# Hybrid mixer and product-key expert layer on one core: three old pairs of expert rows leave the chain of the first picks, in block 1 towards the mixer and in block 7 to behind it

## The chip, the cores and the metric

The kernel is one program on one core of a Trainium2 chip. The metric is the device time of one execution, in microseconds. All arithmetic is float32.

## The reference, cut to what matters

The input is 1024 tokens of width 1024. A mixer (sliding-window attention in one half, gated DeltaNet in the other) gives x1 by a layer norm, and then each token retrieves experts:

```python
def one_block(xb):                                  # 128 tokens
    q = (xb @ w_query).reshape(L, PEER_HEADS, 2, PEER_QUERY_DIM // 2)
    s = jnp.einsum('lhpd,hpkd->lhpk', q, sub_keys)  # 8 heads x 2 lists of 128 keys
    vals, idx = lax.top_k(s, K)                     # 16 best of each list
    cand = (vals[..., 0, :, None] + vals[..., 1, None, :]).reshape(L, PEER_HEADS, K * K)
    ...
    best, pos = lax.top_k(cand, K)                  # 16 best of 256 candidates
    expert = jnp.take_along_axis(cidx, pos, axis=-1)
    gate = jax.nn.softmax(best, axis=-1)
    u = expert_u[expert]                            # 8 heads x 16 picks = 128 rows a token
    v = expert_v[expert]
    h = jax.nn.gelu(jnp.einsum('ld,lhkd->lhk', xb, u), approximate=False)
    return jnp.einsum('lhk,lhkd->ld', (h * gate).astype(xb.dtype), v)
```

A second layer norm over x1 and this sum gives the output.

## The kernel before, in words

The tokens are worked on in NB = 8 blocks of 128 (blocks 0 to 7). For each block n the routine `mix(n, ...)` runs on four engines, each in its own fixed order:

- the mixer proper: rope, attention scores, softmax, convolution taps, the powers and merges that solve the triangular system, the state update (`ws0`, `kv0`, `ws1`, `kv1`), the output projection (`out0` to `out3`), and the first layer norm (`scale1`, `shift1`, `x1_T`);
- the query product: eight chunks of the query weights on PE (line 641), in four parts of two chunks, each followed by a product with the sub-keys (line 1018);
- the picks: DVE takes the 16 best of each key list and the 16 best of the candidates (lines 1547 to 1562), for four groups of lists, numbered 0 to 3. Group 0, "the first picks", ends with the expert numbers of the first 32 slots being written into `expert_used` (line 1906, which raises the semaphore `staged`).

A block has 128 slots, that is PAIRS = 64 pairs. For each slot GpSimd issues one indirect DMA (line 567) that brings 128 rows of u and v, 8 KB each, into one of the RING = 10 places of `ring`. So 5 pairs are on their way or waiting at once, and the gather of slot j waits until slot j - 10 has been added into the sum (`added`); the gathers of a new block wait for `staged` as well. A pair is then worked off in three steps: DVE takes two products with x1 (line 1933), ACT applies gelu and gate and writes two small diagonal matrices (lines 1398 to 1405), PE adds the pair into `expert_sum` (line 1062, 8 products).

The pairs of a block are spread over the work of the block itself and of the next one. Each named point of `mix` is a mark; a table says how many pairs are worked off at it. Marks up to `pick0` take "old" pairs, those of block n - 1 (`EARLIER`); from `top1` on they take "own" pairs, of block n (`OWN`, 15 of them; 23 in block 0, 30 in block 7). DVE and ACT take the pairs of a mark at the mark, PE takes them up to one pair less (`experts(n - 1, b - 1)`) and the last one in `turn_over`. So the order of all work around the picks is a table written by hand:

```python
scale1=1, shift1=1, x1_T=1, half_q=1, qu0=1, top0=1, more0=1, sel0=1, rest0=1, pick0=1,
...
FEWER = ("scores", "softmax", "att_o", "pow2", "solve", "kv0", "dn", "out1")
SECOND_EARLIER = {name: count - (name in FEWER) for name, count in EARLIER.items()}
```

`EARLIER` has 49 old pairs and serves blocks 2 to 7; `SECOND_EARLIER` has 41 and serves block 1, since block 0 works off 23 of its own. The order of DVE from there on is: pair of `half_q`; pair of `qu0`; wait for the first key scores (line 1344, ACT); first half of the 16 best; pair of `top0`; second half; pair of `more0`; candidates and first half of their 16 best; pair of `sel0`; second half; pair of `rest0`; expert numbers, `staged`; pair of `pick0`; then `turn_over`, which waits until PE has added the last old pair, reads the sums (line 1951) and sets x1 in place for the own pairs. PE's order is: query chunks 0 and 1 with the first key scores; then at the marks of the same names: `qu0`, query chunks 2 and 3, `top0`, key scores, `more0`, chunks 4 and 5, `sel0`, key scores, `rest0`, chunks 6 and 7, `pick0`, key scores, `turn_over`. ACT copies each result on between PE and DVE, in the same order. SP loads the weights in halves of a chunk, 512 KB, into four places (line 523); a load waits until the half four places before it has been used. After the query weights of a block SP goes on with weights for the input projection of the next blocks (`pass_steps`); block 7 has none.

With 64 pairs in a block, the last old pair is pair 64; the marks `half_q`, `qu0`, `top0`, `more0`, `sel0`, `rest0`, `pick0` take pairs 58 to 64 before the change.

Of the kernel before, what the change touches and what calls it, by code (L numbers as in the profile page):

```python
# [30 lines left out]
NB = SEQ // P  # L31
# [93 lines left out]
def constants():  # L125
# [24 lines left out]
EARLIER = dict(  # L150
    rope=1, gates=1, taps1=1, scores=2, taps2=1, softmax=2, turn_p=2, att_o=2,
    norms=1, decay=1, kk=1, aT=1, pow2=2, pow4=1, pow8=1, prod3=1, turn32=1, merge32=1, turn64=1,
    merge64=1, solve=2, ws0=1, kv0=2, ws1=1, kv1=1, dn=2, o_T=1, out0=1, out1=1, out2=1, out3=1,
    scale1=1, shift1=1, x1_T=1, half_q=1, qu0=1, top0=1, more0=1, sel0=1, rest0=1, pick0=1,
)
# [3 lines left out]
OWN = {name: 1 for name in ("top1",) + NEXT_IN + AFTER_IN}  # L159
LAST_OWN = {name: 2 for name in OWN}  # L160
FIRST_OWN = {name: 2 if name in ("top1", "more1", "sel1", "rest1", "pick1", "top2", "sel2", "pick2") else 1 for name in OWN}
FEWER = ("scores", "softmax", "att_o", "pow2", "solve", "kv0", "dn", "out1")
SECOND_EARLIER = {name: count - (name in FEWER) for name, count in EARLIER.items()}


def own_of(n):
# [1 line left out]


def earlier_of(n):  # L170
    return SECOND_EARLIER if n == 1 else EARLIER


assert sum(EARLIER.values()) + sum(OWN.values()) == PAIRS and 2 * sum(OWN.values()) <= PART
assert sum(SECOND_EARLIER.values()) + sum(FIRST_OWN.values()) == PAIRS and 2 * sum(FIRST_OWN.values()) <= 2 * PART

# [5 lines left out]
class Marks:  # L182
# [3 lines left out]
    def __init__(self, n, earlier=None, own=None, behind={}):  # L186
        self.names, self.behind, self.own_pairs, self.earlier_pairs = list(EARLIER) + list(OWN), behind, own_of(n), earlier_of(n)
        self.earlier, self.own, self.done = earlier, own, sum(own_of(n - 1).values()) if n else 0
# [1863 lines left out]
```

## Time and profile before

| | |
|---|---|
| time, median of 3 runs | 3087.7 us (3087.36 to 3089.36) |
| the profiled execution | 3080.46 us, its span 3078.7 us |
| busy: PE, DVE, ACT, POOL | 76%, 73%, 37%, 39% of the span |
| indirect gathers | 1024, 1073.81 MB, 84.3% of the 16 DMA engines' time |
| weights and other loads | 154.58 MB, 12.7% |
| all DMA | 1235.90 MB, mean 401 GB/s over the span |

The DMA engines are busy nearly all of the span and no engine is; so a reader looks first for the stretches where the DMA engines were not busy, and for what the gathers waited for there. All times given as "at 494.49" are us from the start of the span.

### The profile page before, as it was taken

The page shows a single profiled execution, that of the slowest core. Times are in us where ns is not written, and L with a number is a line of the kernel's source. Part 1 is how long each engine was busy: PE and PEld are TensorE (multiplying, and loading weights), DVE is VectorE, ACT ScalarE, POOL GpSimd, SP SyncE. Part 2 cuts the span into 40 slices and gives each one's busy share as a digit, 9 for nine tenths or more (in the row PEclk, how much of TensorE's full clock was granted, in tenths as well). Part 3 has the DMA queues.
Part 4 walks back from the last instruction along what each step waited for, and adds up shares of the span by engine and source line. Part 5 has one row for each costly group of instructions (what it writes and reads, how often), then busy time and mean ns, then how long its engine had stood idle before and what let it go on. Part 6 is the DMA issues. An engine that isn't in the chain of part 4 may idle for free.

```text
span 3078.7 us, 37919 instructions
## 1 busy us (share of the span) xinstructions
PE 2348.2 (76%) x11834; PEld 1325.7 (43%) x11834; DVE 2241.4 (73%) x5663; ACT 1127.5 (37%) x3546; POOL 1188.6 (39%) x1028
## 2 busy tenths in 40 slices
PE   8987888867798777877778787876878767775555
PEld 7764445524365343543345343542435434341111
DVE  5577766986679765897658966698657976678644
ACT  4233533354323633235323353324432263323222
POOL 0042452345433353234532445234443344434442
PEclk9999899879899898988989889998988889887777
DMA  8199999999999999999999999999999999999997
GB/s 352 68 401 418 420 420 399 411 415 420 420 417 417 410 421 420 396 413 419 420 419 407 418 419 420 404 406 412 420 420 402 418 416 420 420 378 421 421 421 318
DMA packets 189144, 1235.90 MB, mean 401 GB/s; under 512 B 21768, under 2 KB 21896, under 8 KB 54800
## 3 DMA queue, kind: packets, MB, share of 16 engines
q0 software_dynamic: 147456, 1073.81, 84.3%
q1 hardware_dynamic: 39312, 154.58, 12.7%
q10 hardware_dynamic: 2176, 5.10, 0.4%
q8 instruction: 95, 1.56, 0.2%
q14 instruction: 105, 0.86, 0.1%
HBM read 1229.21 MB, written 4.19 MB: 401 GB/s over the span
## 4 chain that ended last, share of the span: by engine, by line
DVE 30%; PE 29%; DMA 25%; ACT 7%; issue 7%; POOL 3%; DVEq 0%; SPq 0%; POOLq 0%; ACTq 0%
DMA ring<-in_uv,expert_used 24%; DVE ring L1933 13%; PE expert_sum L1062 13%; PE bank L641 7%; POOL ring L567 3%; PE bank L648 2%; ACT diag L1405 2%; PE bank L630 2%; DVE arena L1547 1%; DVE conv L1567 1%; DVE arena L1866 1%; DVE arena L1869 1%; DVE arena L1562 1%; ACT arena L1196 1%; DVE arena L1556 1%
## 5 line engine op out<-in xcount | busy, mean ns | idle before, releaser
L567 POOL DMA_INDIRECT ring<-in_uv,expert_used x1024 | 1188.4, 1161 | 1857.8 <-PE expert_sum L1062 1378.5
L1062 PE MATMUL expert_sum<-ring,diag 128*64 128x512 f32 x4096 | 1187.9, 709 | 632.2 <-ACT diag L1405 631.3
L1933 DVE CUSTOM_DVE_ANT_0 ring<-ring,x_pair 128x1024 f32<-128x1024 f32 x1024 | 1225.9, 1222 | 461.5 <-DMA ring<-in_uv,expert_used 456.9
L1062 PEld LDWEIGHTS expert_sum<-ring,diag 128*64 128x64 f32 x4096 | 311.5, 155 | 1255.9 <-issue 1241.2
L1398 ACT ACTIVATE h_raw<-h_raw 128x2 f32<-128x2 f32 x512 | 104.1, 203 | 1443.4 <-DVE h_raw L1933 1442.1
L1405 ACT ACTIVATE diag<-const,h_raw 128x64 f32<-128x64 f32 x1024 | 292.8, 333 | 9.2 <-PE expert_sum L1062 9.1
L1401 ACT ACTIVATE h_raw<-h_raw,gate_used 128x1 f32<-128x1 f32 x1024 | 245.6, 286 | 16.7
L641 PEld LDWEIGHTS bank<-oT,chunk 128*128 128x128 f32 x1344 | 152.7, 192 | 22.7 <-issue 22.7
L641 PE MATMUL bank<-oT,chunk 128*128 128x128 f32 x1344 | 158.6, 277 | 0.0
L1547 DVE MAX8 arena<-arena 128x8 f32<-128x128 f32 (+1 forms) x384 | 104.2, 325 | 31.2 <-ACT arena L1344 25.1
L630 PE MATMUL bank<-chunk,oT 128*128 128x256 f32 x464 | 109.7, 387 | 0.0
L630 PEld LDWEIGHTS bank<-chunk,oT 128*128 128x128 f32 x464 | 85.6, 190 | 40.5 <-issue 30.3
L641 PEld LDWEIGHTS bank<-o_cat,chunk 128*128 128x128 f32 x768 | 92.2, 200 | 22.1 <-issue 22.1
L1398 ACT ACT_TABLE_LOAD x76 | 97.5, 1283 | 3.6 <-DVE h_raw L1933 2.3
L648 PEld LDWEIGHTS bank<-arena 128*128 128x128 f32 x640 | 78.9, 198 | 41.6 <-issue 38.2
L641 PE MATMUL bank<-o_cat,chunk 128*128 128x128 f32 x768 | 96.6, 286 | 0.0
L648 PE MATMUL bank<-arena 128*128 128x128 f32 x640 | 88.6, 289 | 1.3 <-ACT arena L1289 0.6
L1339 ACT COPY arena<-bank 128x512 f32<-128x512 f32 (+1 forms) x33 | 18.9, 573 | 180.5 <-PE bank L641 180.5
L1933 DVE DVE_READ_ACCUMULATOR2_ANT h_raw<- 128x1 f32 x1024 | 83.5, 82 | 0.0
L1567 DVE SCALAR_TENSOR_TENSOR conv<-conv_in,conv_w,conv 128x128 f32<-128x128 f32 x288 | 77.6, 342 | 0.0
L641 PEld LDWEIGHTS bank<-xT_even,chunk 128*128 128x128 f32 x576 | 67.1, 195 | 13.8 <-issue 13.8
L641 PE MATMUL bank<-xT_even,chunk 128*128 128x128 f32 x576 | 70.1, 281 | 0.0
(289 smaller groups left out, 2652.4 us busy)
## 6 DMA issues: line engine op xcount, KB each, us to landing
chunk<-in_weights SPq DMA_DIRECT2D x228, 512.0 KB, 8.4
ring<-in_weights SPq DMA_DIRECT2D x17, 1024.0 KB, 23.5
ring<-in_uv,expert_used POOLq DMA_INDIRECT x1024, 15.2
chunk<-in_weights SPq DMA_DIRECT2D x4, 1024.0 KB, 20.5
x<-in_x SPq DMA_DIRECT2D x8, 512.0 KB, 14.9
o_cat<-in_xT SPq DMA_DIRECT2D x7, 512.0 KB, 14.1
out<-oT ACTq DMA_DIRECT2D x7, 512.0 KB, 9.3
xT_even<-in_xT SPq DMA_DIRECT2D x4, 512.0 KB, 10.2
```

The lines of the kernel that those rows point to most:

```text
L567: pool.indirect_dma_start(out=place(n, j), out_offset=None, in_=io["uv"], in_offset=bass.IndirectOffsetOnAxis(ap=expert_used[:, j:j + 1], ...
L630: mm = pe.matmul(out, act[:, k, :], w[:, k % 4, :], start=(k == ks[0]), stop=(k == ks[-1]))
L641: mm = pe.matmul(out, w[:, k % 4, i * P:(i + 1) * P], act[:, k, :], start=(k == 0), stop=(k == KT - 1))
L648: mm = pe.matmul(out[:, hs], lhsT[:, hs], rhs[:, hs], start=True, stop=True)
L1062: mm = pe.matmul(expert_sum[i][c * SPAN:(c + 1) * SPAN, :], diag[:, (j % DIAGS) * SPAN:(j % DIAGS + 1) * SPAN], place(n, j)[:, D + i * 512 ...
L1196: act.activation(pr, pr, ACT.Exp, bias=col(S_NMAX + h), accum_out=col(S_SUM + h)).then_inc(probs.sem, 1)
L1398: act.activation(h_raw[:, pair[0]:pair[1] + 1], h_raw[:, pair[0]:pair[1] + 1], ACT.Gelu).then_inc(gelued.sem, 1)
L1401: act.activation(h_raw[:, j:j + 1], h_raw[:, j:j + 1], ACT.Copy, scale=gate_used[:, j:j + 1]).then_inc(weighted.sem, 1)
L1405: act.activation(diag[:, (j % DIAGS) * SPAN:(j % DIAGS + 1) * SPAN], C["halves"], ACT.Copy, scale=h_raw[:, j:j + 1]).then_inc(diag_ready.s ...
L1547: ins = dve.max(values[:, one[part]], one[2])
L1567: stt(out=convo[:, t, :], in0=conv3[n % 2][:, t, k:k + P], scalar=conv_w[:, t * TAPS + k:t * TAPS + k + 1], in1=convo[:, t, :], op0=ALU.mu ...
L1933: dve.tensor_tensor_reduce(u, u, x_pair[:, (j % 2) * D:(j % 2 + 1) * D], 1.0, 0.0, ALU.mult, ALU.add, h_raw[:, j:j + 1]).then_inc(dotted.s ...
```

## The change

Two tables are changed, and nothing else: no instruction is added or removed, only the places of pairs of lines 1933, 1398 to 1405 and 1062 in the engines' orders change.

```diff
-FEWER = ("scores", "softmax", "att_o", "pow2", "solve", "kv0", "dn", "out1")
+FEWER = ("softmax", "att_o", "solve", "dn", "out1", "qu0", "more0", "rest0")
 SECOND_EARLIER = {name: count - (name in FEWER) for name, count in EARLIER.items()}
+
+
+LAST_EARLIER = dict(EARLIER, qu0=0, more0=0, rest0=0, pick0=4)
+assert sum(LAST_EARLIER.values()) == sum(EARLIER.values())
...
 def earlier_of(n):
-    return SECOND_EARLIER if n == 1 else EARLIER
+    return SECOND_EARLIER if n == 1 else LAST_EARLIER if n == NB - 1 else EARLIER
```

In block 1 the marks `scores`, `pow2` and `kv0` of the mixer take 2 pairs in place of 1, and `qu0`, `more0` and `rest0` take none; `top0`, `sel0` and `pick0` then take pairs 62, 63 and 64. In block 7 the mixer is as before up to pair 58 at `half_q`; `qu0`, `more0` and `rest0` take none, `top0` and `sel0` take pairs 59 and 60, and `pick0`, behind `staged`, takes the four pairs 61 to 64. Blocks 0 and 2 to 6 are unchanged.

## Rows read from the trace of the kernel before

**Rows 1.** The page: busy share and rate of the DMA engines in 40 slices, gather queue.
```profile
DMA  8199999999999999999999999999999999999997
GB/s 352 68 401 418 420 420 399 411 415 420 420 417 417 410 421 420 396 413 419 420 419 407 418 419 420 404 406 412 420 420 402 418 416 420 420 378 421 421 421 318
...
q0 software_dynamic: 147456, 1073.81, 84.3%
```
**Rows 2.** Stretches: length; busy us of PE, PEld, DVE, ACT, POOL; PE clock, DMA share, GB/s.
```profile
411.00:491.00 80.00, 62.80 (x295) 32.82 (x295) 50.14 (x95) 27.65 (x96) 33.02 (x30) 0.87 1.01 420
...
520.00:540.00 20.00, 15.78 (x96) 10.50 (x96) 15.92 (x41) 6.17 (x15) 9.11 (x9) 0.97 0.93 346
540.00:580.00 40.00, 29.52 (x112) 17.27 (x112) 38.32 (x131) 11.68 (x38) 10.11 (x10) 0.80 1.01 421
580.00:600.00 20.00, 20.00 (x103) 13.75 (x102) 19.04 (x62) 6.06 (x27) 5.56 (x7) 1.00 0.98 383
...
2730.00:2740.00 10.00, 9.68 (x72) 7.39 (x73) 7.63 (x22) 5.51 (x13) 3.21 (x4) 1.00 0.32 111
```
**Rows 3.** Timeline of DVE in block 1's state update: start, length, line, idle before.
```profile
414.38 1.23 DVE L1933 CUSTOM_DVE_ANT_0 ring<-ring,x_pair 128x1024 f32<-128x1024 f32 x1 [1.25 <-DMA ring<-in_uv,expert_used]
...
416.87 1.23 DVE L1933 CUSTOM_DVE_ANT_0 ring<-ring,x_pair 128x1024 f32<-128x1024 f32 x1 [0.53 <-DMA ring<-in_uv,expert_used]
```
**Rows 4.** Timeline of DVE from block 1's first key scores to the reading of sums.
```profile
494.49 0.87 DVE L1547 MAX8 arena<-arena 128x8 f32<-128x128 f32 x4 [2.90 <-ACT arena L1344]
...
502.32 1.22 DVE L1933 CUSTOM_DVE_ANT_0 ring<-ring,x_pair 128x1024 f32<-128x1024 f32 x1
...
507.18 0.75 DVE L1848 TENSOR_TENSOR arena<-arena 128x256 f32<-128x256 f32 x2
...
513.53 1.22 DVE L1933 CUSTOM_DVE_ANT_0 ring<-ring,x_pair 128x1024 f32<-128x1024 f32 x1 [1.62 <-DMA ring<-in_uv,expert_used]
...
516.83 1.23 DVE L1933 CUSTOM_DVE_ANT_0 ring<-ring,x_pair 128x1024 f32<-128x1024 f32 x1
...
521.75 0.18 DVE L1857 TENSOR_SCALAR arena<-arena 128x32 uint32<-128x32 uint32 x1
...
526.81 0.72 DVE L1906 CAST expert_used<-arena 64x16 uint32<-64x16 f32 x4
...
533.41 2.78 DVE L1951 SCALAR_TENSOR_TENSOR oT<-x_pair,expert_sum 64x512 f32<-64x512 f32 x4 [2.94 <-PE expert_sum L1062]
```
**Rows 5.** Timeline of PE in the same stretch of block 1.
```profile
493.65 1.94 PE L1062 MATMUL expert_sum<-ring,diag 128*64 128x512 f32 x8
495.52 3.84 PE L641 MATMUL bank<-oT,kept 128*128 128x128 f32 x32
...
519.85 7.41 PE L641 MATMUL bank<-oT,chunk 128*128 128x128 f32 x64
527.19 1.94 PE L1062 MATMUL expert_sum<-ring,diag 128*64 128x512 f32 x8
...
531.32 1.94 PE L1062 MATMUL expert_sum<-ring,diag 128*64 128x512 f32 x8 [1.10 <-ACT diag L1405]
```
**Rows 6.** Timeline of POOL: the first new gather of block 1.
```profile
528.44 1.17 POOL L567 DMA_INDIRECT ring<-in_uv,expert_used  x1 [20.39 <-DVE expert_used L1906]
```
**Rows 7.** Timeline of PE in block 7 behind the last query products: pairs 63 and 64.
```profile
2735.48 1.94 PE L1062 MATMUL expert_sum<-ring,diag 128*64 128x512 f32 x8
2737.35 1.16 PE L1018 MATMUL bank<-sub_keys,arena 128*128 128x128 f32 x8
2738.83 1.94 PE L1062 MATMUL expert_sum<-ring,diag 128*64 128x512 f32 x8 [0.32 <-ACT diag L1405]
```
**Rows 8.** Timeline of POOL in block 7: first new gather, first one released by an own pair.
```profile
2735.88 1.16 POOL L567 DMA_INDIRECT ring<-in_uv,expert_used  x1 [19.50 <-DVE expert_used L1906]
...
2758.64 0.94 POOL L567 DMA_INDIRECT ring<-in_uv,expert_used  x1 [9.80 <-PE expert_sum L1062]
```
**Rows 9.** One microsecond of block 7 around the restart of the DMA engines.
```profile
2737.00:2738.00 1.00, 1.00 (x7) 0.65 (x6) 0.84 (x5) 0.96 (x4) 0.69 (x2) 1.00 0.60 82
```

## The prediction

> **What bounds the kernel now.** I read the page first, then stretches, then the timelines of the four engines around the first picks. The page [rows 1] shows DMA engines at nine tenths or more in all slices from the fourth on but the last, at about 420 GB/s, while no compute engine passes 76%. So after block 0 the kernel ends when 1236 MB have been moved, and the time is that plus the stretches in which the DMA engines had too little to do. The reader should see how little that is: the stretches [rows 2] give 1.01 at 420 GB/s through block 1's mixer, and full rate in 540 to 580. In block 1 around the first picks (520 to 540) the rate is 346 GB/s, which costs 20 x (420 - 346) / 420 = 3.5 us. In block 7 (2730 to 2740) the share is 0.32 and 10 x (1.01 - 0.32) = 6.9 us are lost. These are the holes that the change can fill: 10.4 us together, 0.34%. 0.2% is 6.2 us, about what a measurement of this kernel can tell from no change; more than half of both holes must close before it is faster by more.
>
> One gather takes 2.49 us: in the mixer the second gather of a pair and the first of the next reach DVE 2.49 us apart, each after a wait for DMA [rows 3], and 1.049 MB (1073.81 / 1024) at 420 GB/s is 2.50. A pair is 5.0 us. The important point is what DVE's wait means: the pair itself comes late. DVE isn't idle there for want of work that could be put in.
>
> **Block 1, three pairs to the mixer.** At `kv0` DVE has now to see three pairs more before it goes on. The DMA engines are full throughout [rows 2], so these pairs come 6 x 2.49 = 14.9 us later than the ones that stood there, and no slack of DVE helps. The extra pair at `scores` and that at `pow2` cost part of it sooner, but from the state update on DVE follows the DMA, so the sum is the same. All later marks to `half_q` also take pairs with numbers higher by three. The first norm, x1, the query products and the first key scores move by 14.9: DVE begins its picks at 494.49 + 14.9 = 509.4 instead of 494.49 [rows 4].
>
> From there the chain is shorter. On DVE: before, from 494.49 to the end of the write of `expert_used` at 526.81 + 0.72 = 527.53, 33.0 us. The pair of `more0` goes (502.32 to 507.18: 4.86), that of `rest0` (516.83 to 521.75: 4.92), and the wait of 1.62 for `sel0`'s pair, which will have landed. The pair of `qu0` gives nothing: DVE waited for the key scores behind it anyhow (2.90). 33.0 - 11.4 = 21.6, so `staged` comes at 509.4 + 21.6 = 531.0, 3.5 later than before.
>
> On PE the gain is smaller. The query products fill it: one pair takes 495.52 - 493.65 = 1.87 [rows 5], and three fewer stand before the last query products, 5.6 us. PE is 14.9 - 5.6 = 9.3 late at their end, 527.19 + 9.3 = 536.5. The last old pair needs ACT, which copies the last queries before it gets to that pair, so it comes 4.1 behind (531.32 - 527.19) as now, and the reading of the sums (line 1951), at 533.41 now, moves to 542.7. Queued behind this wait are the staging of x1 and all own pairs, and for their `added` wait the gathers.
>
> Does that reach the end? After 533 DVE is busy 38.3 of 40 us and then 19.0 of 20, without a wait to absorb a delay, and at 580 to 600 the DMA engines run short for the second time, 383 GB/s [rows 2]: there the gathers wait for DVE's pace, so a DVE that is 9.3 late makes them 9.3 late. The DMA's own account agrees. The first new gather comes 3.5 after 528.44 [rows 6]; and four half chunks of input weights (512 KB, 1.25 us each) that fill the stretch behind 519.85 + 2 today can only be asked for when the last query products have begun, 9.3 later, so they no longer fill the hole: 3.5 + 5.0 = 8.5 us less moved. I take **+9.3**; bounds are 3.5 (only the first gathers' delay, should the loads find their place elsewhere) and 14.9 (nothing won in the chain).
>
> **Block 7, three pairs behind the first picks.** Up to the first key scores nothing changes. DVE writes `expert_used` some 10 us sooner. But a new gather needs a place too: the first new one takes that of pair 60, and PE now adds 60 at `pick0`, behind the last query products. These end at 2735.48 [rows 7] less three pairs, 5.6, so 2729.9. The first half of pair 60 is in after three quarters of its 1.94, 1.5 us, and the queue starts 0.9 behind its release (527.53 to 528.44, [rows 4, 6]): 2732.3, against 2735.88 today [rows 8]. So the hole gets shorter by 3.6, not by 6.9: its end is set by PE instead of DVE. The gathers of the old pairs 63 and 64 are released later as well, by the 7.3 us of two query chunks and by 8.4 (two chunks and the key scores); I take it that the queue still lasts to 2731.0, as today (2737.9 less the 6.9), which these rows can't settle.
>
> Then PE. At 2729.9 pair 60; pairs 61 to 64 wait for ACT, which must first copy the last queries and load gelu's table, as today (2735.48 to 2738.83, 3.35): 61 begins at 2733.2, then 62 and 63 (3 x 1.87 for the three), key scores 1.1, pair 64 1.94: 2741.8, against 2740.8 today [rows 7]. The last old pair ends **1.1 later**. Everything of DVE's turn-over is behind it, so the first gather released by an own pair moves from 2758.64 to 2759.7 [rows 8]. Today the ten new gathers reach the DMA engines from 2737.9 on (share 0.60 in 2737 to 2738 [rows 9]; 2.0 behind their issue), last 24.9, until 2762.8, and the next, effective at 2760.6, is in time by 2.2. After, ten gathers from 2734.3 last until 2759.2 and the next is effective at 2761.7: a new hole of 2.5. Gain 3.6 - 2.5 = 1.1. I take **-1.1**; bounds 6.9 won (the hole closed, no new one) and 1.1 lost (DVE's delay sets the rest).
>
> The Trainium skill ("DMA: Bandwidth & Descriptors", section "Anatomy of one DMA — SWDGE (gpsimd) path") gives a DMA 2.0 us plus its bytes at 436 GB/s, and puts most of the 2.0 behind the last byte. By the 436 a gather in a full queue takes 2.41 us and block 1's delay becomes 14.4, half a microsecond less; rows 3 show 2.49 and the row decides. Rows 9 show the engines still not full 2 us after the issue, so here the delay lies ahead of the data, and it reopens after each hole.
>
> **The sum.** 3080.46 + 9.3 - 1.1 = 3088.7 for the profiled execution, +8.2. The profiled execution is 7.2 under the median of the runs, and I put the difference on the median: 3087.7 + 8.2 = **3095.9**, slower by 0.27%.
>
> **Rivals.**
> 1. *Slower as above*, 55%. For it: the DMA share of 1.01 before the picks [rows 2, 3], DVE without idle time behind them. Own range 3091 to 3099.
> 2. *Block 1 is paid only in part*, 29%. If the gathers, not DVE, set the pace at 580 to 600, or the input weights still find idle engines, block 1 costs 3.5 to 6, and if block 7's new hole doesn't open its gain is 3.6. Sum 0 to +5: 3088 to 3093, no change that can be told. Against it: 19.0 of 20 us busy on DVE with the DMA at 383 GB/s.
> 3. *Faster: the mixer takes the three pairs for nothing*, 12%. DVE's idle time in 411 to 491 is 80 - 50.1 = 29.9 us, and three pairs need 3 x 2.3 = 6.9 of it. If they had landed by then, x1 would not be late, `staged` would come up to 11.4 sooner and the hole of 3.5 would close; with block 7's 6.9 fully won the time is 3087.7 - 10.4 = 3077.3, and with PE's limit there 3083. It decides whether gathers wait in the ring or DVE waits for gathers: a wait for DMA before the second gather of nearly each pair [rows 3] speaks against it.
> 4. *Worse*, 4%: query chunks come late for a PE that is earlier within its chain, and pair 63 or 64 opens a hole in block 7. Two or three late half chunks at 1.25 us each, 3 to 4 more, 3099 to 3102.
>
> **How the numbers follow.** Likeliest is 1, so 3095.9. The range goes down into 2 and partly 3, and up to where 4 begins: 3084 to 3100, leaving about one in ten below and one above. Faster by over 0.2% (under 3081.5) is the part of 3 in which both holes close, 0.09; slower (over 3093.9) is four fifths of 1, 4, and a little of 2: 0.56; within, the rest, 0.35.
>
> **What would show it.** In block 1: the first key scores reach DVE near 509 and `expert_used` is written near 531; line 1951 runs near 542.7; a hole in the DMA share between about 524 and 533, longer than today. If x1's picks begin before 500, step one is wrong. In block 7, counted from its first key scores: `expert_used` 10 us sooner, the first gather released by PE and not by DVE, line 1951 about 1 later, and two short holes in place of one. If the start of the picks is late but blocks 2 to 6 begin less than 8 us late, the delay was absorbed where I say DVE has no slack.

## The result and the profile after

The changed kernel takes 3102.2 us (median of 10 runs, 3093.49 to 3109.69) against 3088.55 us for the kernel before in the same session (10 runs, 3086.65 to 3092.91). The ratio is 1.0044 with a 95% interval of 1.0036 to 1.0052, so the change costs 13.6 us, between 11.1 and 16.1. The forecast was +8.2. In the experiments below one execution, of the run with three pairs behind the picks, took 5458.52 us and is left out of its figures.

The profiled execution of the changed kernel has a span of 3101.6 us, 22.9 more than the span of before. This is more than the runs show, and a marker explains a part. The work up to about 190 us is the same in both kernels. ScalarE's copy in that stretch that follows an idle time of 8.42 us starts at 187.50 in the profile of before:

```profile
187.50 0.59 ACT L1133 COPY conv_in<-bank 128x512 f32<-128x512 f32 x1 [8.42 <-PE bank L641]
```

and in the profile after at 192.93:

```profile
192.93 0.59 ACT L1137 COPY conv_in<-bank 128x512 f32<-128x512 f32 x1 [8.42 <-PE bank L645]
```

It is 5.43 us later in code that the change doesn't touch. So one profile can't be held against another by its raw times. Below, "net" means that a profile's own lateness at this marker has been taken off: 5.43 here. In four of the runs below block 1 is unchanged, and there line 1951 of block 1 is net between 0.2 early and 0.8 late: so well does the marker serve in block 1. In the new file lines are numbered 4 higher: 1951 is 1955, 1062 is 1066, 641 is 645, 567 is 571.

Stretches of the profile after; columns as in [rows 2]. The first two answer to 520 to 540 there and the last three to 2730 to 2740. The third and fourth are new: line 1951 of block 1 is 17.6 us later in this profile than in that of before, and 17.6 us ahead of them, from 547 to 567, the profile of before has 419 GB/s.

```profile
525.00:540.00 15.00, 15.00 (x124) 13.50 (x125) 12.75 (x38) 3.74 (x9) 3.04 (x3) 1.00 0.49 153
540.00:545.00 5.00, 3.55 (x24) 1.98 (x22) 0.00 (x0) 0.70 (x2) 2.81 (x3) 1.00 0.98 378
565.00:575.00 10.00, 10.00 (x38) 5.25 (x35) 9.32 (x32) 3.56 (x9) 2.70 (x3) 0.83 0.85 322
575.00:585.00 10.00, 8.12 (x38) 5.50 (x38) 9.72 (x28) 2.40 (x11) 4.21 (x4) 1.00 0.97 354
2740.00:2750.00 10.00, 9.55 (x75) 7.85 (x75) 9.79 (x22) 3.75 (x9) 2.34 (x2) 1.00 0.96 366
2750.00:2760.00 10.00, 8.60 (x50) 4.17 (x48) 4.27 (x11) 6.40 (x22) 3.67 (x4) 1.00 0.55 205
2780.00:2790.00 10.00, 6.60 (x26) 2.03 (x24) 9.61 (x30) 4.90 (x14) 6.13 (x5) 0.84 0.85 303
```

The reader should see three things. In block 1 the hole has grown from 3.5 us to 15 x (420 - 153) / 420 = 9.5 us in 525 to 540 alone. Behind it a second one has opened: 10 x (420 - 322) / 420 = 2.3 us and 10 x (420 - 354) / 420 = 1.6, so 3.9 in all. In block 7 one hole has become two: 10 x (420 - 205) / 420 = 5.1 and 2.8, and 1.3 ahead of them, 9.2 in all, where 2730 to 2740 lost 7.4 before [rows 2].

The timeline of VectorE in block 1, which answers to [rows 4]: first key scores, `expert_used`, and the reading of the sums.

```profile
514.03 0.87 DVE L1551 MAX8 arena<-arena 128x8 f32<-128x128 f32 x4 [7.27 <-ACT arena L1348]
...
534.66 0.72 DVE L1910 CAST expert_used<-arena 64x16 uint32<-64x16 f32 x4
...
551.05 2.78 DVE L1955 SCALAR_TENSOR_TENSOR oT<-x_pair,expert_sum 64x512 f32<-64x512 f32 x4 [12.74 <-PE expert_sum L1066]
```

The timeline of TensorE in the same place, which answers to [rows 5]:

```profile
541.53 1.94 PE L1066 MATMUL expert_sum<-ring,diag 128*64 128x512 f32 x8
544.92 1.16 PE L1022 MATMUL bank<-sub_keys,arena 128*128 128x128 f32 x8 [1.45 <-issue]
547.51 3.40 PE L1066 MATMUL expert_sum<-ring,diag 128*64 128x512 f32 x8 [1.44 <-ACT diag L1409]
```

The timelines of ScalarE and GpSimd there: the copy of the last queries, then the first new gather, the seventh, and the eleventh.

```profile
544.28 0.58 ACT L1343 COPY arena<-bank 128x512 f32<-128x512 f32 x1 [7.67 <-remote]
```
```profile
536.28 1.17 POOL L571 DMA_INDIRECT ring<-in_uv,expert_used  x1 [31.20 <-DVE expert_used L1910]
...
545.81 0.94 POOL L571 DMA_INDIRECT ring<-in_uv,expert_used  x1 [2.16 <-remote]
...
568.92 1.07 POOL L571 DMA_INDIRECT ring<-in_uv,expert_used  x1 [15.10 <-PE expert_sum L1066]
```

Net, the first key scores are 514.03 - 494.49 - 5.43 = 14.1 us late, `expert_used` 2.4, the end of the last query products (taken by the pair behind them, 541.53 against 527.19) 8.9, and line 1955 is 551.05 - 533.41 - 5.43 = 12.2 late. Up to the query products this is the chain as forecast. Behind them ScalarE's copy, which needs nothing but these products, starts 2.75 us after them; in the profile of before it starts 0.11 after:

```profile
527.30 0.59 ACT L1339 COPY arena<-bank 128x512 f32<-128x512 f32 x1 [2.70 <-PE bank L641]
```

The second hole shows how line 1951 sets the pace. The ring has ten places, so ten new gathers can go out and the eleventh waits until the first own pair has been added, which is work behind line 1951. In the profile of before it goes out here:

```profile
551.39 1.07 POOL L567 DMA_INDIRECT ring<-in_uv,expert_used  x1 [10.16 <-PE expert_sum L1062]
```

That is 17.98 us behind line 1951, and in the profile after 568.92 - 551.05 = 17.87: the eleventh gather has moved with line 1951, net 12.1 later, while the first has moved by 2.4, and the DMA engines run short between them.

Block 7 in the profile after, TensorE and then GpSimd. This answers to [rows 7, 8]. Block 6's line 1955 is 19.92 us later than its line 1951 was before (2392.93 against 2373.01), and that is to be taken off here ("net" in block 7).

```profile
2727.03 2.94 PE L645 MATMUL bank<-oT,chunk 128*128 128x128 f32 x24 [0.36 <-DMA chunk<-in_weights]
...
2734.58 2.94 PE L645 MATMUL bank<-oT,chunk 128*128 128x128 f32 x24 [0.76 <-issue]
...
2748.98 2.94 PE L645 MATMUL bank<-oT,chunk 128*128 128x128 f32 x24 [0.45 <-DMA chunk<-in_weights]
2751.85 1.94 PE L1066 MATMUL expert_sum<-ring,diag 128*64 128x512 f32 x8
2755.19 5.37 PE L1066 MATMUL expert_sum<-ring,diag 128*64 128x512 f32 x24 [1.41 <-ACT diag L1409]
2760.49 1.16 PE L1022 MATMUL bank<-sub_keys,arena 128*128 128x128 f32 x8
2761.58 1.94 PE L1066 MATMUL expert_sum<-ring,diag 128*64 128x512 f32 x8
```
```profile
2754.59 0.94 POOL L571 DMA_INDIRECT ring<-in_uv,expert_used  x1 [8.17 <-PE expert_sum L1066]
```

The last query products end at 2751.85 - 19.92 = 2731.9 (forecast 2729.9), the first new gather goes out at 2734.7 (forecast 2732.3), and line 1955, at 2763.77, is 2.9 later than before (forecast 1.1). The query products have three short waits, 1.57 us together; two of them end with a half chunk of weights, and for the one of 0.76 the trace names no releaser.

### The profile page after: what moved, and what is told of

The parts are those of the page before. It is cut to its first block, busy times and chain, and to the rows that moved or that the text cites. A ratio compares the mean times of both kernels' runs of the same rounds, so it can differ in the third digit from the quotient of the medians.

```text
span 3101.6 us, 37919 instructions
## 1 busy us (share of the span) xinstructions
PE 2339.2 (75%) x11834; PEld 1324.3 (43%) x11834; DVE 2241.3 (72%) x5663; ACT 1127.8 (36%) x3546; POOL 1194.8 (39%) x1028
## 4 chain that ended last, share of the span: by engine, by line
DVE 31%; DMA 27%; PE 25%; ACT 7%; issue 6%; POOL 2%; another core or an unknown queue 1%; ACTq 0%; DVEq 0%; POOLq 0%; SPq 0%
DMA ring<-in_uv,expert_used 25%; DVE ring L1937 14%; PE expert_sum L1066 11%; PE bank L645 6%; POOL ring L571 2%; ACT diag L1409 2%; DMA chunk<-in_weights 2%; PE bank L634 2%; DVE arena L1551 1%; DVE conv L1571 1%; PE bank L652 1%; PE bank L783 1%; DVE arena L1870 1%; DVE arena L1873 1%; DVE arena L1566 1%
## 5 line engine op out<-in xcount | busy, mean ns | idle before, releaser
L1405 ACT ACTIVATE h_raw<-h_raw,gate_used 128x1 f32<-128x1 f32 x1024 | 245.6, 286 | 16.7
```

The lines of the kernel that those rows point to most:

```text
L1405: act.activation(h_raw[:, j:j + 1], h_raw[:, j:j + 1], ACT.Copy, scale=gate_used[:, j:j + 1]).then_inc(weighted.sem, 1)
```

## The experiments

All were timed in turns with the kernel before on the same chip. The change in us is the ratio's excess over 1 times the median of before, with the ratio's 95% interval. The last column is how much later line 1951 comes in the profile, net of the marker (in the rows for block 2 or 7: how much longer it takes from the block before).

| run | change in us | line 1951 later by |
|---|---|---|
| block 1 alone | +12.4 (8.6 to 16.4) | 12.9 |
| block 7 alone | +2.2 (-0.6 to 4.9) | 4.0 |
| both again | +13.0 (9.0 to 17.0) | 9.8 and, in block 7, 3.4 |
| block 1, three pairs behind | +3.1 (0.3 to 5.6) | 4.1 |
| block 1, one pair to the mixer | +4.6 (1.9 to 7.4) | 5.0 |
| block 7, `qu0` kept | +1.5 (-1.2 to 4.3) | 3.9 |
| block 1, more in the chain | +2.2 (-0.6 to 4.9) | 3.7 |
| block 7, more in the chain | +4.3 (1.5 to 7.1) | 4.9 |
| block 2, three pairs to the mixer | +7.7 (4.3 to 11.1) | 13.6 |
| block 1, the other three | +12.7 (8.6 to 16.7) | 16.1 |
| all blocks, two at `rest0` | +41.1 (36.4 to 45.7) | 5.8 in block 1, 42.0 by block 7 |
| block 1, gathers held back | +9.6 (5.9 to 13.3) | 7.9 |

The last column has scatter too. In block 1 it is the 0.2 early to 0.8 late of the first section. From block 6 to block 7 seven profiles with an unchanged block 7 take 0.1 to 2.0 us longer than the profile of before (1.0 in the mean), so the values for block 7 are rather 1 us too high. From block 1 to block 2 eleven profiles with an unchanged block 2 differ from it by -0.9 to +5.2.

**The change, cut in two.** Block 1's table alone:

```diff
-FEWER = ("scores", "softmax", "att_o", "pow2", "solve", "kv0", "dn", "out1")
+FEWER = ("softmax", "att_o", "solve", "dn", "out1", "qu0", "more0", "rest0")
```

> Block 1's edit alone (three old pairs from qu0, more0, rest0 back to scores, pow2, kv0); block 7 as before. Theory A (each pair put into block 1's mixer delays the first picks by its own DMA time, 14.9 us for three, of which PE gives back 5.6; DVE carries the rest to the end): 9 to 12 us slower than before, most of the measured 13.7; first key scores on DVE 14 to 15 later. Rival B (the excess is block 7's): under 6 us slower. Rival C (the excess comes from stalls elsewhere that the profiled run of the changed kernel happened to have, such as 5 us in block 0): about 8 to 9 us slower in the median, with a scatter of 10 us from run to run.

Block 7's table alone:

```diff
+LAST_EARLIER = dict(EARLIER, qu0=0, more0=0, rest0=0, pick0=4)
-    return SECOND_EARLIER if n == 1 else EARLIER
+    return SECOND_EARLIER if n == 1 else LAST_EARLIER if n == NB - 1 else EARLIER
```

> Block 7's edit alone (three old pairs behind the first picks); block 1 as before. Theory A (the hole's end moves from DVE to PE, and the last old pair ends about 1 later): -1.5 to +1.5 us. Rival B (late query half chunks and the longer row of old pairs behind the picks cost what is missing in the forecast): +3 to +5 us. Rival D (the hole of 6.9 us closes): -4 to -7 us.

The changed kernel once more:

> The changed kernel once more, beside the two halves on one chip. If the two edits are independent, its difference is the sum of the two others within 2 us. Theory C (a part that differs from execution to execution) expects the profile's share in block 0, 5 us in the first one, to be another size or absent here, and a scatter of 10 us again.

Measured: 3099.41, 3089.45 and 3098.53 us against 3087.03. The two parts add up (12.4 + 2.2 = 14.6 against 13.0 and 13.6). Of theory C the scatter is there: the changed kernel's runs spread over 16.2 us in the first session and 9.1 in this one, those of before over 6.3 and 9.9, and the lateness at the marker is 1.60 us here. But both sessions give the same change, so scatter isn't what makes it. So block 1 carries nearly all. Its term looks larger than 9.3, but its interval begins at 8.6, so the time alone doesn't show it. Block 7 is no gain; its interval reaches from -0.6 up, so a gain of 1.1 is outside it. In the profile of block 7 alone TensorE waits 1.14 and 0.75 us for half chunks:

```profile
2714.56 2.94 PE L642 MATMUL bank<-oT,chunk 128*128 128x128 f32 x24 [1.14 <-DMA chunk<-in_weights]
...
2722.10 2.94 PE L642 MATMUL bank<-oT,chunk 128*128 128x128 f32 x24 [0.75 <-DMA chunk<-in_weights]
```

**Block 1 with the pairs behind the picks.** The mixer of block 1 is as before, and block 1 gets what block 7 got:

```diff
 SECOND_EARLIER = {name: count - (name in FEWER) for name, count in EARLIER.items()}
+SECOND_EARLIER.update(qu0=0, more0=0, rest0=0, pick0=4)
```

> Block 1 with the three pairs of qu0, more0 and rest0 moved behind the picks (pick0 takes four) and the mixer as before; block 7 as before. Theory A (the cost of the change lies in the mixer; behind the picks only PE's order counts): first key scores on DVE at 494 as before, line 1951 about 1 us later, time -1 to +2 us. Rival B (taking pairs out of the chain is what costs, by late query chunks and a starved DMA): +5 us or more, as with the mixer.

Measured 3089.26 us, +3.1. That is a little above theory A's range, and rival B's +5 is still within the interval; against B, the interval doesn't meet that of block 1 alone. Line 1951 is 4.1 late where A had 1: TensorE waits 0.67, 0.72 and 0.71 us in its query products, so these end only 529.12 - 527.19 - 3.53 = 1.6 us sooner, net, and not 5.6. A chain with the same three marks empty costs 3 here and 12 with the pairs in the mixer. So it is the place in the mixer that costs, not the emptied chain.

**One pair.** Only `qu0`'s pair goes back to the mixer, at `scores`:

```diff
-FEWER = ("scores", "softmax", "att_o", "pow2", "solve", "kv0", "dn", "out1")
+FEWER = ("softmax", "att_o", "pow2", "solve", "kv0", "dn", "out1", "qu0")
```

> Block 1 alone, and only one pair moved: that of qu0 goes back to the mixer, at scores; block 7 as before. Theory A (each pair put ahead of the first picks makes them 5.0 us later, and PE gets 1.9 back): the first key scores about 5 us later than before, the last query products and line 1951 some 3 us later, and the time +3 to +4 us, a third or a quarter of the +12.4 of all three. Rival B (the cost is a stall that comes only when the last query products meet the first new gathers, as in the three profiles with all three pairs in the mixer): no such stall here, the time +0 to +1. Rival C (DVE's slack takes the first pair): the first key scores no later than 2 us, time +0.

Measured 3090.97 against 3088.11: +4.6, a little over a third of the three. The first key scores come at 501.20, net 4.0 late, the last query products 2.5 late. C falls. B doesn't, as to its cause: it expected no stall here, but there is one, and it makes up most of the 5.0 us by which line 1951 is late. ScalarE's copy of the last queries is on time. Then its copy of the key scores behind them, which end by 535.35, starts at 538.11, and line 1951 waits 3.46 us more behind the last pair, in by 537.6:

```profile
541.07 2.78 DVE L1951 SCALAR_TENSOR_TENSOR oT<-x_pair,expert_sum 64x512 f32<-64x512 f32 x4 [9.47 <-remote]
```

**Block 7 with `qu0`'s pair left.**

```diff
+LAST_EARLIER = dict(EARLIER, more0=0, rest0=0, pick0=3)
```

> Block 7 alone, with the pair of qu0 left in its place and only those of more0 and rest0 behind the picks (pick0=3). Theory A (in block 7 PE gains only what the arrival of the query chunks lets it gain; the three pairs taken out leave waits of 1.14 and 0.75 us for a chunk): the pair of qu0 fills a wait, the last query products end at most 1 us later than with all three moved, the last old pair 1 us earlier, and the time is +0 to +1.5 us against before. Rival B (all pairs on PE count in full): the last query products end 1.9 later than with all three moved, time +1 to +2.5. Rival C: the whole of what block 7 cost in the earlier run is scatter, and the time is within 1 us of before for both.

Measured +1.5, which doesn't tell it from +2.2 or from nothing. Its profile speaks for rival B as to TensorE: counted from block 6's line 1951 the last query products end 1.7 later than in block 7 alone (2745.91 - 2384.26 against 2738.94 - 2378.94), a pair in full. The two chunk waits of block 7 alone are gone, and in their place stands one of 2.34 us within the last query products; the first two new gathers had gone out at 2736.18 and 2737.65, before that half chunk was in.

```profile
2741.41 4.57 PE L642 MATMUL bank<-oT,chunk 128*128 128x128 f32 x24 [2.34 <-DMA chunk<-in_weights]
```

**The reverse, in block 1 and in block 7.** Three more pairs leave the mixer and stand in the chain:

```diff
+SECOND_EARLIER.update(turn_p=1, pow4=0, kv1=0, qu0=2, more0=2, rest0=2)
```

> The reverse of the change in block 1: three more pairs taken out of the mixer (at turn_p, pow4 and kv1) and put in the chain of the first picks, two each at qu0, more0 and rest0. Theory A (the sum for a moved pair holds in both directions): the first picks begin 14.9 us sooner, the last query products 9.3 sooner, expert_used 3.5 sooner; the hole between the last old and the first new gather closes, 2 to 4 us won. Rival B: the pairs in the chain have not landed when DVE comes to them, expert_used is written no sooner and all stays within 1 us. Rival C: DVE waits in the chain for pairs that are late, and the picks end later than before, +2 to +5 us.

```diff
+LAST_EARLIER = dict(EARLIER, scores=1, pow2=1, kv0=1, qu0=2, more0=2, rest0=2)
```

> The reverse of the change in block 7: three pairs taken out of the mixer (at scores, pow2 and kv0) and put in the chain, two each at qu0, more0 and rest0. Theory A: expert_used 3.5 sooner and the last old pair earlier as well, so the hole of 6.9 us shrinks by 2 to 4 us without a new one behind it; time -2 to -4 us. Rival B: the pairs have not landed when DVE comes to them; expert_used comes no sooner, within 1 us. Rival C: DVE waits for late pairs in the chain and expert_used comes later, +1 to +5 us.

Measured +2.2 and +4.3; neither is faster. In block 1 the picks begin 489.38 - 494.49 - 4.47 = 9.6 us sooner, but VectorE then waits seven times for a gather in the chain, up to 2.75 us and 13.4 us together, and `expert_used` is written 1.9 net later. The sum for a moved pair doesn't hold backwards: a pair that the DMA engines have not brought can't be worked off wherever it stands. A falls; C describes both runs, and in block 1 the time fits B as well.

**The same move in block 2.**

```diff
+THIRD_EARLIER = dict(EARLIER, scores=3, pow2=3, kv0=3, qu0=0, more0=0, rest0=0)
-    return SECOND_EARLIER if n == 1 else EARLIER
+    return SECOND_EARLIER if n == 1 else THIRD_EARLIER if n == 2 else EARLIER
```

> Block 2 alone gets what the change does to block 1: three more pairs in its mixer (a third one each at scores, pow2 and kv0), none at qu0, more0 and rest0; block 1 and block 7 as before. Theory A (the sum 14.9 less 5.6 holds for any block whose mixer is full of DMA): line 1951 of block 2 comes 9.3 later after that of block 1 than before (366.9 us there), and the time is +9 to +10. With it, theory A1: the wait of 2 to 3 us, in which no one is released by TensorE and which all four kernels with pairs moved into block 1's mixer show in block 1, is tied to block 1, and doesn't show here; A2: it comes with the move, shows in block 2 too and the time is +11 to +13. Rival B (block 1 is special because its picks follow block 0's many own pairs): block 2 costs less than 5.

Measured 3097.01 against 3088.74, +7.7. Block 1 is not special: the time is above B's 5 but for the end of its interval, and the late release shows in block 2, where ScalarE's copy comes 2.72 us behind the start of the pair at 907.72. The wait is A2's, the time is rather A1's (+11 is the interval's very end): of the 13.6 us by which line 1951 is late in block 2 (8 to 15, by the scatter above), 3.1 are gone at block 3, where none of the other twelve profiles is more than 0.2 us quicker than before. Here something is given back that block 1 doesn't give back; why stays open.

```profile
910.44 0.59 ACT L1340 COPY arena<-bank 128x512 f32<-128x512 f32 x1 [7.63 <-remote]
```

**Another three pairs of block 1.**

```diff
+FEWER = ("softmax", "att_o", "solve", "dn", "out1", "top0", "sel0", "pick0")
```

> Block 1 alone: the three pairs that go to the mixer are those of top0, sel0 and pick0, in place of qu0, more0 and rest0. Theory A (the cost follows line 1951, which waits for the last old pair on TensorE): the last old pair is now that of rest0 and is done ahead of the last query products, so line 1951 waits for expert_used only. The first key scores are 14.9 later, expert_used 14.9 less two pairs of 4.9 on DVE, 5.1 later; line 1951 at about 533, no later than before. If the time follows line 1951 alone: +0 to +2. If it follows the first new gather (5.1 later): +5. Rival B (what costs is the late start of the picks with all that hangs on it, whatever TensorE does): +9 to +12 as with the other three.

Measured +12.7. My premise was wrong. TensorE works one pair behind the marks and takes the last in `turn_over`, so an old pair stands behind the last query products even when `pick0` has none: it starts at 548.52, and line 1951 comes at 552.38, net 16.1 late. The pair of `pick0` stood behind the products, so TensorE gets back two pairs ahead of them and not three (they end net 12.3 late), and the late release is the longest of all, 3.46 us. The first new gather is only 3.1 late; the time is near that of line 1951 and far from that of the gather. So the cost doesn't follow the first gather, and the value that I gave for line 1951 was wrong. Between theory A's line 1951 and rival B, the late start of the picks (net 14.5 here), this run can't choose: both would give such a time. The next run does.

**One pair of all blocks moved from `pick0` to `rest0`.**

```diff
-    scale1=1, shift1=1, x1_T=1, half_q=1, qu0=1, top0=1, more0=1, sel0=1, rest0=1, pick0=1,
+    scale1=1, shift1=1, x1_T=1, half_q=1, qu0=1, top0=1, more0=1, sel0=1, rest0=2, pick0=0,
```

> All blocks: the last old pair stands at rest0 (two there) and none at pick0, so TensorE has no old pair behind its last query products. DVE gets 2.4 to 4.9 us more work ahead of expert_used, and line 1951 no longer waits 2.9 us for the last old pair. Theory A (a block's price follows line 1951 and the first new gather alike): expert_used 2.5 later and line 1951 at most as late as before; time within 0.1 % of before up to +2.5 a block. Rival B (line 1951 alone sets the pace): up to 1 us a block sooner, -2 to -7 in all. Rival C (the first gather alone): 2.5 to 4.9 a block, +17 to +34.

Measured 3129.73, +41.1, 5.9 for each of seven blocks; even above rival C. The last gathers have not landed when VectorE wants them at `rest0` (it waits 2.34 us there), and `expert_used` comes 6.5 net later in block 1 and line 1951 5.8; here too a pair stands behind the last query products. From block 1 to block 5 line 1951 loses another 5.5 a block, and in block 7 it is 2787.07 - 2740.91 - 4.14 = 42.0 net late. Line 1951 and the time agree again. The picks of block 1 begin 1.7 us sooner, net (496.98 against 494.49, less 4.14), and the kernel is slower all the same: what costs is not the start of the picks by itself.

**Gathers held back.** Block 1 alone as above, and GpSimd waits before block 1's first new gather until the last queries have been copied:

```diff
                             pool.wait_ge(*staged.at(n, i + 1))
+                            if n == 1 and i == 0:
+                                pool.wait_ge(*queries_c.at(1, len(picks_of(1))))
```

> As block 1 alone (three pairs in its mixer), and GpSimd waits ahead of block 1's first new gather until ScalarE has copied the last queries of the first half, so no new gather is in flight while TensorE makes the last query products. Theory S (the 2 to 3.5 us in which no engine is released by TensorE, seen in each kernel with pairs in the mixer, comes from new gathers in flight at the end of the last query products): no such wait here, ACT's copy starts 0.04 us behind the last query products. The first gather is 5 to 6 us later, so the time is +12 to +17 all the same. Rival T (it comes from the late start of the picks itself): the wait of 2 to 3.5 us is there as well, the first gather comes 8 to 9 us later, and the time is +15 to +21.

Measured 3096.97 against 3088.27, +9.6. ScalarE, TensorE and GpSimd:

```profile
538.17 0.59 ACT L1341 COPY arena<-bank 128x512 f32<-128x512 f32 x1 [5.02 <-PE bank L643]
```
```profile
538.06 1.94 PE L1064 MATMUL expert_sum<-ring,diag 128*64 128x512 f32 x8
539.93 1.16 PE L1020 MATMUL bank<-sub_keys,arena 128*128 128x128 f32 x8
541.40 1.94 PE L1064 MATMUL expert_sum<-ring,diag 128*64 128x512 f32 x8 [0.32 <-ACT diag L1407]
```
```profile
539.64 0.94 POOL L569 DMA_INDIRECT ring<-in_uv,expert_used  x1 [37.70 <-ACT arena L1341]
```

The copy starts 0.11 us behind the products again, the last pair takes 1.94 us, and line 1951's counterpart runs at 543.49, net 7.9 late in place of 12.9. Theory S holds in that holding back the gathers removes the late release. As to the time, +9.6 lies below its +12 to +17 (the interval reaches into it): the first new gather goes out 539.64 - 534.20 + 3.38 - 2.22 = 6.6 us later than in block 1 alone, and nothing is lost by it. The stretches say why: the first hole is longer, but the second, behind it, is closed. From 565 to 585 this profile has 419 GB/s, where block 1 alone has 333, which is 20 x (420 - 333) / 420 = 4.1 us. The median is 2.4 us below that of block 1 alone, each against its own before 2.8; the two intervals overlap, so that the time itself is better is not shown, only that it is not worse.

No kernel tried was faster than the one before.

## Why the prediction was wrong in size

**Block 1, start of the picks: right.** +14.9 forecast; net 14.1 in the profile after, 13.8 and 14.1 in the two others with all three pairs moved. The rate in the mixer stays at 420 GB/s and VectorE can't absorb a pair there. Rival 3 is out.

**Block 1, chain on VectorE and TensorE: right.** `expert_used` +3.5 forecast, 2.4, 2.1 and 2.4 net measured. End of the last query products +9.3 forecast, 8.9, 8.6 and 9.2 measured. The chain behind the products is 0.8 shorter than I had it (538.17 to 541.40 in the run with held gathers, 3.2 us, against 4.0 before), since VectorE isn't late with its pair any more. Without anything else line 1951 would be 7.9 late, as the run with the gathers held back shows.

**Block 1, "the last old pair comes 4.1 behind as now": this step failed.** I read the distance from the profile of before, where the new gathers go out after the last query products end (528.44 against 527.19). With the picks' chain shortened on VectorE more than on TensorE, the first new gathers go out while TensorE is still in these products: five, 1.24 us apart, from 536.28 to 541.47 in the profile after. In this situation ScalarE sees TensorE's products 2.0 to 3.0 us late (at 544.28 in the profile after), and GpSimd goes on only at 545.81, 2.3 us behind the end of the pair that it waits for. The old pair begins 547.51 - 541.53 = 5.98 us behind the products in place of 4.1, and line 1951 comes 9.5 behind their end in place of 6.2. TensorE, without work, then runs the last pair in 3.36 to 3.40 us instead of 1.94 in two of the three profiles. The account for the profile after, counted over the same chain and so no test of it, is 8.9 + 2.6 (late release) - 0.8 + 1.5 (slow pair) = 12.2, which is the shift measured; for block 1 alone 9.2 + 3.0 - 0.8 + 1.4 = 12.8 (12.9), for both again 8.6 + 2.0 - 0.8 + 0 = 9.8 (9.8). The test is the run with the gathers held back. It takes the late release and the slow pair away and leaves 7.9; that it also makes the time shorter lies within the intervals.

**Block 1, "does that reach the end": right.** The shift of line 1951 in the profile after is 17.6 in block 1, 18.6 in blocks 2 and 3, 19.5, 19.1, 19.9 in blocks 4 to 6. Nothing is given back (with block 7 alone it also grows, from 3.3 in block 1 to 5.9 in block 6, so that growth is not the change's). Rival 2 is out. But the second account, 3.5 us for the first gathers and 5.0 for the half chunks, was a coincidence of sums: with the first gather 9.0 us net later instead of 2.4 the time is no worse. It also left out the second hole, which I drew up for block 7 and not for block 1: in the profile after 3.9 us are lost there. What sets the price is line 1951, by way of the eleventh gather, which goes out 17.5 to 18.1 us behind it in block 1 of twelve of the fourteen profiles and 19.2 in the two others. In the table shift and time agree for eleven of twelve runs within 3.5 us (block 2 is the exception), where the intervals are some 3 to 5 us wide to each side.

**Block 7, "-1.1": wrong in sign, and too small a loss to be sure of by itself** (+2.2, -0.6 to 4.9). The structure is as forecast: `expert_used` sooner (2743.59 - 19.92 = 2723.7 against 2734.26), the first new gather released by TensorE, two holes. The step that failed is "these end at 2735.48 less three pairs, 5.6". TensorE got 3.5 us (3.0 and 2.5 in the two other profiles), not 5.6, since it comes to its query chunks before they are in (1.57 us of waits for the 2.1 missing in the profile after): this is the first half of rival 4, which I gave 4%, with waits of 0.36 to 1.14 us where I had 1.25 for each. The 2.1 us are found again in the first gather, which wins 1.2 instead of 3.6, and in line 1955, 2.9 to 4.0 late instead of 1.1 (rather 1.9 to 3.0, by the scatter of unchanged blocks 7).

**The sum.** By the runs of the parts it is +12.4 + 2.2 against my 9.3 - 1.1: by these values about half of the miss is block 1's, in the late release and the slow pair, and half block 7's, in the query chunks. The intervals of the parts are wide enough for another split. The direction and rival 1's mechanism held. The range ended too low: no case of mine let anything be added behind block 1's query products, and rival 4 was held for rare where its waits show in all three profiles with block 7's edit.

## What to carry to other kernels

When a move shortens the chain of one engine more than that of another, read again which of the two events comes first at their meeting point; a distance taken from the old profile holds only in the old order. Where the DMA engines are full, a pair put ahead of a point delays it by its full transfer, but a pair taken away from there gains nothing that hasn't been brought by then. And with several holes, ask which event the end follows: here it is the reading of the sums, not the first new gather: the ring's places are used up by ten gathers, and the eleventh waits for work behind that reading. A late first gather and a late eleventh one are two holes that trade against each other.

## What the runs showed that was not expected

**A late release.** In 98 blocks (1 to 7 of 14 profiles) ScalarE's copy of the last queries starts 0.04 us behind the modelled end of the query products, with five exceptions: 2.68 in the changed kernel, 2.03 in its second run, 3.04 with block 1 alone, 2.65 with block 2 and 3.46 with the other three pairs. A sixth case is the run with one pair, in which this copy is on time and those behind it are late. All six are in the block whose mixer got more pairs, and in all six the first new gathers had gone out 2.8 to 8.0 us before the query products ended. In block 7 with `qu0` kept two new gathers go out 9.7 us ahead of that end and nobody is released late, but TensorE itself waits 2.34 us for a half chunk. Those who wait are ScalarE, GpSimd and VectorE, and the trace mostly names their releaser "remote". Holding the gathers back removes it. In that run the four half chunks of input weights are asked for from 533.76 on, while the query products run, and the copy is on time: the loads alone don't do it.

It isn't bound to a pause of the gathers either. In the mixer VectorE waits for another result of TensorE (line 1759, 1763 in the new file), and at 745.54 in the profile after it starts 1.7 us behind the modelled end of it, 743.82:

```profile
740.88 2.94 PE L652 MATMUL bank<-arena 128*128 128x128 f32 x24
745.54 0.69 DVE L1763 TENSOR_TENSOR arena<-arena,bank 128x512 f32<-128x512 f32 x1 [5.79 <-remote]
```

The DMA share is 1.01 from 735 to 745 and no weights are being loaded. The same line is released that late, by "remote", in 15 cases in seven of the profiles, changed blocks or not; the profile of before has none (0.04 us at 728.08). Why results of TensorE arrive late I can't say: TensorE's own records go on without a gap meanwhile.

**TensorE's clock on a single pair.** Behind such a wait, and behind idle times of 3.39 and 3.27 us in the two runs with more in the chain, the granted clock drops from the upper level (2.4 GHz, 1.00 in 540 to 545) towards the lower one (1.2 GHz) in part of the cases, and a pair then takes 3.36 to 3.68 us instead of 1.94. In the profile after, the stretch of the slow pair (columns as above) has a mean of 0.60; TensorE had idled 1.45 and 1.44 us ahead of it:

```profile
547.00:551.10 4.10, 3.59 (x9) 1.10 (x10) 0.05 (x1) 0.84 (x3) 0.93 (x1) 0.60 1.01 421
```

In the second run of the changed kernel the idle times are 0.80 and 1.44 us and the pair takes 1.94.

**The first 190 us vary.** The marker of the first section stands at 187.50 in the profile of before and between 189.10 and 192.93 in the thirteen others, with the same code. The profile of before is the earliest of them, and its execution, 3080.46 us, is 8.1 below the median of its kernel. That is a good part of why the two profiles differ by 22.9 us where the runs differ by 13.6; the prediction added its +8.2 to the median and not to this execution, and so is not touched by it.
